# Two sets of split weights instead of three, and an expert unit held from the middle of the sections, in a one-layer mixer and mixture-of-experts kernel

## What is computed

```python
h  = RMSNorm(x) * (1 + scale_mix) + shift_mix          # scale, shift, gate from SiLU(c) @ w_ada
z  = h @ w_in              # [sc_x | sc_B | sc_C | u | v | gate_A | gate_B], 7 x 1024 columns
yA = sc_B * causal_dwconv3(sc_C * sc_x)
yB = GELU(u) * (tril(W_s) @_chunk LN(GELU(v)) + b_s)
x  = x + gate_mix * ((sigmoid(gate_A) * yA + sigmoid(gate_B) * yB) @ w_out)
h  = RMSNorm(x) * (1 + scale_ffn) + shift_ffn
x  = x + gate_ffn * MoE(h)         # top-4 of 32 experts, clamped SwiGLU, width 1024
```

## Time and profile before

| | before |
|---|---|
| median of 3 runs | 1135.45 us |
| the profiled execution's own time | 1135.09 us |
| its span, first to last instruction | 1133.3 us |
| granted TensorE clock, mean | 0.965 |
| PE busy / DVE busy / ACT busy | 960 / 369 / 230 us |
| moved by DMA, mean rate | 466.79 MB, 412 GB/s |

### The profile page before, as it was taken

The page is one execution under the profiler, slowest core; times in us unless marked ns, Lnnn a source line. Parts: engine busy times, 40 slices in busy tenths (PEclk is TensorE's granted clock), DMA queues, the critical chain, the costliest instruction groups (busy, mean ns, idle before and its releaser), DMA issues.

```text
span 1133.3 us, 24456 instructions
## 1 busy us (share of the span) xinstructions
PE 959.9 (85%) x10066; PEld 512.4 (45%) x10067; DVE 369.0 (33%) x844; ACT 230.4 (20%) x324; POOL 8.3 (1%) x30
## 2 busy tenths in 40 slices
PE   7999999998987897699798898988978688687665
PEld 5799999833332343243343333334333233233221
DVE  3688897642221221122221222212221121121112
ACT  3644534611110110011110111101110010010002
POOL 0010000000000000000000000000000000000000
PEclk9999999999999999999999999999999899899987
DMA  9999899999999999999999999999999999999996
GB/s 358 396 354 366 310 370 363 418 427 429 428 429 427 428 428 429 427 428 428 429 427 428 428 429 427 428 426 430 426 429 429 428 429 426 429 428 429 426 427 277
DMA packets 55854, 466.79 MB, mean 412 GB/s; under 512 B 4756, under 2 KB 5844, under 8 KB 27284
## 3 DMA queue, kind: packets, MB, share of 16 engines
q1 hardware_dynamic: 55568, 466.12, 99.1%
q10 hardware_dynamic: 260, 0.30, 0.1%
HBM read 465.35 MB, written 1.05 MB: 412 GB/s over the span
## 4 chain that ended last, share of the span: by engine, by line
PE 54%; DMA 37%; SPq 4%; issue 3%; DVE 1%; ACT 0%; DVEq 0%; another core or an unknown queue 0%; PEldq 0%; ACTq 0%
PE B L1530 26%; DMA trio<-in_w_down_dram 25%; PE B L1225 14%; DMA W<-in_w_down_dram 6%; DMA W<-in_w_gate_up_dram 4%; PE B L1554 3%; PE B L1479 2%; PE B L1543 2%; SPq L486 2%; SPq L490 1%; PE B L1304 1%; PE B L1485 1%; DMA raw<-in_w_ada_dram 1%; PE B L1255 1%; PE B L1313 1%
## 5 line engine op out<-in xcount | busy, mean ns | idle before, releaser
L1530 PE MATMUL B<-W,trio 128*32 128x512 f32 (+1 forms) x4768 | 470.8, 530 | 124.6 <-DMA W<-in_w_gate_up_dram 51.2
L1530 PEld LDWEIGHTS B<-W,trio 128*32 128x32 f32 x4768 | 155.6, 111 | 366.8 <-issue 222.4
L1155 DVE TENSOR_SCALAR EW<-B 128x256 f32<-128x256 f32 x46 | 19.5, 424 | 438.0 <-PE B L1530 438.0
L769 ACT ACTIVATE EW<-EW 128x256 f32<-128x256 f32 x46 | 19.2, 417 | 678.3 <-DVE EW L1155 678.3
L1225 PE MATMUL B<-hh,wh 128*128 128x256 f32 x384 | 109.1, 284 | 0.0
L1225 PE MATMUL B<-hl,wh 128*128 128x256 f32 x384 | 108.7, 283 | 0.0
L1225 PE MATMUL B<-hh,wl 128*128 128x256 f32 x384 | 108.6, 283 | 0.0
L1554 PE MATMUL B<-EW,trio 32*128 32x256 f32 x752 | 67.1, 426 | 8.7 <-PE B L1554 7.8
L1225 PEld LDWEIGHTS B<-hh,wh 128*128 128x128 f32 x384 | 73.7, 192 | 1.7 <-issue 0.8
L1172 DVE TENSOR_TENSOR EW<-B,trio 128x256 f32<-128x256 f32 x46 | 19.5, 424 | 166.6 <-PE B L1530 166.6
L1225 PEld LDWEIGHTS B<-hl,wh 128*128 128x128 f32 x384 | 73.7, 192 | 0.0
(11 more groups left out here) (257 smaller groups left out, 710.9 us busy)
## 6 DMA issues: line engine op xcount, KB each, us to landing
W<-in_w_gate_up_dram SPq DMA_DIRECT2D x112, 2048.0 KB, 34.2
W<-in_w_down_dram SPq DMA_DIRECT2D x48, 2048.0 KB, 37.3
spare<-in_w_gate_up_dram SPq DMA_DIRECT2D x16, 2048.0 KB, 37.1
trio<-in_w_down_dram SPq DMA_DIRECT2D x15, 2048.0 KB, 40.4
raw<-in_w_in_dram SPq DMA_DIRECT2D x10, 2048.0 KB, 13.8
raw<-in_w_ada_dram SPq DMA_DIRECT2D x4, 2048.0 KB, 18.3
raw<-in_w_ada_dram SPq DMA_DIRECT2D x6, 1024.0 KB, 12.1
raw<-in_w_in_dram SPq DMA_DIRECT2D x4, 1024.0 KB, 15.7
```

What stands on the lines that cost most here:

```text
L769: A(sg, gs, ACT.Sigmoid, scale=ALPHA).then_inc(sig_ready, 1)
L1155: V.tensor_scalar(halves(gs), paired(GU[:, 0:QC]), LIMIT, None, ALU.min).then_inc(gmin_ready, 1)
L1530: t = M(o, src[:, k % KQ, CAP * (k // KQ):CAP * (k // KQ) + CAP], w, start=(k == 0), stop=(k == KT - 1))
```

## The change

`SETS` becomes 2. The 16 KB a partition of the third set become a buffer `held`, which in the expert phase is slot 6 of `W`. The first expert unit u0 is loaded into it right after the unit `("in", SC_B, 1)` has been issued, with no wait of its own. All other early expert units move by one place in `PLACE`, each trigger now loads the unit with the next higher number into the same place as before, and the load that waited for `mix_done` 2 is gone (the third set's place is taken already). With two sets every split stands one iteration later against PE: iteration m splits piece m+2 instead of m+3; the piece that was split between the gelus and the squares of V is split in the loop; the split of section piece 1 waits for the whole V product; that of piece 26 waits for `mix_part` 1, that of piece 27 for `mix_done` 2.

```diff
-    SETS = 3
+    SETS = 2
+    HELD = 6
...
     def set_of(q):
-        return (q // 2) % SETS if q < V_ALL else (q - V_ALL + 1) % SETS
+        return (q // 2) % SETS if q < V_ALL else (q - V_ALL) % SETS
...
+            held = sb1("held", [P, UW])
...
-        SET_AT = [RING + set_of(len(piece_of) - 4 + i) for i in range(3)]
-        PLACE = (R2, R3, "spare", R1, R0, 8, 9, SET_AT[1], SET_AT[2], SET_AT[0], 7, "trio")
+        SET_AT = [RING + set_of(len(piece_of) - SETS + i) for i in range(SETS)]
+        PLACE = (HELD, R2, R3, "spare", R1, R0, 8, 9, SET_AT[0], SET_AT[1], 7, "trio")
...
         def set_free(eng, q):
...
-            elif t < 2:
-                eng.wait_ge(v_pair, t + 2)
-            elif t == 2:
+            elif t == 0:
+                eng.wait_ge(v_pair, 3)
+            elif t == 1:
                 eng.wait_ge(v_done, TA * NH)
             elif t < HALVES + SETS:
                 eng.wait_ge(sec_done, t - SETS + 1)
+            elif t == HALVES + SETS:
+                eng.wait_ge(mix_part, 1)
             else:
-                eng.wait_ge(mix_part, 1)
+                eng.wait_ge(mix_done, TA)
...
+                if n == unit_no[("in", SC_B, 1)]:
+                    load(0, 0)
...
             sp.wait_ge(ada_used, ada_units.index(unit_no[("half", 2, 5)]) + 1)
-            load(0, 0)
+            load(1, 0)
             sp.wait_ge(split_l, pieces_before[-4])
-            load(1, 0)
+            load(2, 0)
             sp.wait_ge(ada_used, len(ada_units))
             load_out_half()
             sp.wait_ge(ada_summed, NH)
-            load(2, 0)
+            load(3, 0)
             sp.wait_ge(split_l, pieces_before[-3])
-            load(3, 0)
+            load(4, 0)
             sp.wait_ge(split_l, pieces_before[-2])
-            load(4, 0)
+            load(5, 0)
             sp.wait_ge(sec_done, 2 * NS * NH)
-            load(5, 0)
+            load(6, 1)
             sp.wait_ge(m_ready, NH * 2)
-            load(6, 1)
-            sp.wait_ge(mix_done, TA)
             load(7, 1)
             sp.wait_ge(mix_part, 2)
             load(8, 1)
...
-            piece_high(V_ALL + 2)
             act.wait_ge(v_mu, 1)
...
-                        piece_high(V_ALL + m + 3)
+                        piece_high(V_ALL + m + SETS)
...
             m_high(1, 1)
+            piece_high(len(piece_of) - 2)
             piece_high(len(piece_of) - 1)
...
-            piece_low(V_ALL + 2)
             dve.wait_ge(v_sq, TA)
...
-                        piece_low(V_ALL + m + 3)
+                        piece_low(V_ALL + m + SETS)
...
             m_low(1, 1)
+            piece_low(len(piece_of) - 2)
             piece_low(len(piece_of) - 1)
```

More of the change, by code:

```diff
@@ L414, in _, with load @@
             sp.dma_start(x_sb[:, :, :], x_in[0].rearrange("(a p) n -> p a n", p=P)).then_inc(s_x, 16)
+            def load(u, e):
+                j = u % UNITS
+                if j < NQ:
+                    sp.dma_start(unit_pair(u).rearrange("p g n -> p (g n)"), gu_v[e, j]).then_inc(s_unit[u % SLOTS], 16)
+                elif PLACE[u % SLOTS] == "trio":
+                    sp.dma_start(unit_pair(u), dn_v[e, j - NQ]).then_inc(s_unit[u % SLOTS], 16)
+                else:
+                    sp.dma_start(unit_pair(u).rearrange("p g n -> p (g n)"),
+                                 dn_v[e, j - NQ].rearrange("p g n -> p (g n)")).then_inc(s_unit[u % SLOTS], 16)
             for n, (kind, s, h) in enumerate(units):
@@ L480, in load_out_half @@
                     sp.dma_start(to.rearrange("p (k n) -> p k n", n=HALF), out_v[:, 4 * c:4 * c + 4, HALF:2 * HALF]).then_inc(s_outw[c], 16)
[L482 to L493, removed]
+            assert [home(n) for n in (split_units[-4], split_units[-3], split_units[-2])] == [PLACE[i] for i in (2, 4, 5)]
             sp.wait_ge(ada_used, ada_units.index(unit_no[("half", 2, 5)]) + 1)
-            load(0, 0)
+            load(1, 0)
             sp.wait_ge(split_l, pieces_before[-4])
-            load(1, 0)
+            load(2, 0)
             sp.wait_ge(ada_used, len(ada_units))
```

## The result

The changed kernel took **1154.73 us** (median of 3 runs, 1154.29 to 1154.77) where the kernel before took 1135.45: a ratio of 1.0164 with an interval of 1.015 to 1.0178, or 19.3 us. The direction was forecast, the size was not: 1147.7 was forecast with a range up to 1151.5. The profiled execution took 1154.29 (span 1152.5).

The account below looks back on a forecast made before the run. DMA bytes were taken to set the pace from about 230 us, with PE's chain deciding when the stream starts. Terms (a) to (e), 2.5+0.6+3.7+4.0+1.5 = 12.3 us, on 1135.45 gave 1147.7, range 1142.5 to 1151.5.

Parts of the forecast that it names:

- (e): PE clock lowered after stalls: 1.5 us for work behind the tail's stall, bounds 0 and 1.6; nothing for the first stall.
- (a): Start of the sections: the splits of piece 2 stand behind gelus, squares and root, so PE stalls 2.5 us.
- Rival C: More stalls: first pieces and sections drop the clock too, late halves delay DVE; 4 us more, 1151.7; chance 0.12.
- (b): Before piece 12: DVE's gating and two weighings delay the low split; PE stalls 0.6 us, low 0.2, high 1.
- (c): Pieces 15 to 18: DVE's weighings and convolution work delay low splits; 3.7 us of stalls, between 2.8 and 4.2.
- (d): Tail: the split of piece 27 waits for `mix_done` 2, gates and residual pairs queue behind it; PE stalls 4.0 us.
- (f): The held unit's early 4.9 us of queue only moves the DMA hole: restart at 130.9 and not 125.07.
- (g): Load dropped at `mix_done` 2: queue runs dry near 231.5, PE chain sets the restart; first expert-released unit +12.3 us.
- B: The cover holds: PE never waits, DMA gains and losses net -1.0 to +0.7 us, 1135.4; chance 0.08.
- D: Stalls in the sections only: gates and DVE's tail work fit beside PE's product; 7 us, 1142.5; chance 0.10.

Follow-up runs that it names:

- run 3: Changed kernel with ACT's gate copies ahead of the splits of pieces 26 and 27, and DVE's low split of 27 behind its row work: 1152.56 us.
- run 2: Kernel before, three sets kept, but the first three pieces split under the changed kernel's conditions and order: 1140.52 us, ratio 1.0033.
- run 4: Changed kernel with 30 PE turns whose result nobody reads, ahead of the tail's wait for the residual pairs: 1150.53 us, ratio 1.0121.
- run 5: The changed kernel measured once more, with no edit: 1153.44 us, ratio 1.0164 against the kernel before.
- run 1: Kernel before, three sets kept, only the split of piece 27 waits for `mix_done` 2 and not `mix_part` 1: 1142.62 us, ratio 1.0057.
- run 8: Changed kernel with the held unit's load issued late, just ahead of the next unit's: 1153.11 us, ratio 1.0161.
- run 7: run 6 with high split 1 behind the gelus, high split 2 between squares and root, low ones alike: 1144.03 us, ratio 1.0076.
- run 9: run 7 with the last four half weighings one piece later on DVE: 1140.29 us, ratio 1.0038 against the kernel before.
- run 10: run 7 with DVE's weighings after the first cut to 16 or 64 columns, so it computes something else: 1136.64 us, ratio 1.0013.
- run 11: Kernel before, no held unit, with the load that followed `mix_done` 2 moved behind `mix_part` 2: 1139.05 us, ratio 1.0032.
- run 6: Changed kernel with the tail reordered: half the gate copies ahead of high split 26, half behind; DVE's tail work interleaved with its splits: 1147.38 us.

## Why the forecast had the direction and not the size

**The failed step is (e), the clock**, with the sentence "For the 2.5 us of (a) I take nothing; high end 1.5". The prediction took 1.5 us for a lower clock in all, with 3.0 to 3.1 as its own high end. The changed kernel loses 3.9 to it behind its stalls: 1.4 in the sections (155.31 us, against 153.87 in run 3 with the same stalls at full clock; run 2 has 1.7) and 2.4 after the tail's (17.3 us from the turns to the first expert, for 14.9; run 4 gets 2.3 back). Another 1.5 is lost at the start, which no edit explains, and 0.7 after the last landing.

The profiled execution is 19.2 over before's where 12.3 was forecast. The 6.9 between them are 2.4 of clock behind the stalls (3.9 less 1.5), 2.2 of longer stalls (13.0 by the starts of PE's matmuls, 8.6 and 4.35, for 10.8), 1.5 at the start, and 0.8 from the first expert's release to the end, 0.7 of it the clock in the last product of the kernel. With (e) right and nothing else changed the forecast would have been 1150.1, inside its range. The longer stalls carry that just past its end (1152.3), the start and the end of the kernel do the rest. The start's part is chance as far as the runs show; run 5, without it in its profiled execution, has 1153.44 and lies outside too.

For the tail the prediction took one early window that lost 1.55 us of its five. In run 1, with the same stall, that is the right size: 1.7. In the changed kernel the clock stayed down for longer, with 3.4 us lost over the window of 229 to 239 (0.66 of ten), 2.4 of it on work of PE; its second profiled execution and run 8 show the same (turns of 1.98 us in both). Why the same stall costs 1.7 in one kernel and 2.4 in the other stays open. For the first stall the prediction gave no reason to take nothing. Rival C ("the sections drop the clock too") had that mechanism, with 1151.7, and was given 0.12.

The other steps, one by one:

- (a) First pieces: 2.5 forecast, 2.74 by the row and 2.9 by the starts; run 2 has it alone, run 7 takes it away. Right in place and cause.
- (b) Piece 12: 0.6 forecast, 0.77 measured, within its bounds.
- (c) Pieces 15 to 18: 3.7 forecast as 0.6, 0.45, 0.6 and 2.1 to 2.4; measured 0.65, 0.71, 0.4 and 2.18, which is 3.9 by the brackets and 4.6 by the starts. The places are right; run 9 shows that the largest is the weighing at that place, run 10 that without DVE's bursts 0.3 is left of them. The one of 0.71 stands behind the half that landed late, as the prediction said it might.
- Sections in all: 6.8 forecast, 7.4 by the brackets and 8.6 by run 3, at full clock. Six times the 0.16 that a bracket leaves out is 1.0 of the difference. The product's start is 11.6 later: these 8.6, 1.4 of clock, and 1.5 from the start.
- (d) The tail: 4.0 forecast, 4.19 measured (4.35 by the starts), by the queue order that the prediction named. The rows of ACT and DVE in the changed kernel follow it: high 27, the gates behind it, and DVE between them.

```profile
220.30 1.92 ACT L649 ACTIVATE wh<-trio 128x2048 fp32r<-128x2048 f32 x1 [3.27 <-PE B L1229]
222.12 5.20 ACT L730 ACTIVATE tmp<-mod 32x512 f32<-32x512 f32 x8
...
222.25 2.29 DVE L851 TENSOR_TENSOR wl<-trio,wh 128x2048 fp32r<-128x2048 f32 x1 [2.89 <-ACT wh L649]
224.46 0.23 DVE L1018 COPY cols<-B 128x8 f32<-128x8 f32 x2
...
229.76 0.68 DVE L1046 TENSOR_TENSOR HV<-B,tmp 128x512 f32<-128x512 f32 x1
```

- (f) The hole moves and doesn't close: forecast restart 131, measured 134.56. The forecast moved it by one piece (5.8) and left out PE's own delay. That was 5.9 at the end of piece 11, and 3.7 of it came through. Run 8 can't tell the early load's worth from nothing, as forecast.
- (g) What the held unit saves is spent when the load of `mix_done` 2 is gone, and the chain sets the restart: the first load on the dry queue is issued at 238.9 and lands 8.9 later as forecast, and the stream is late by PE's lateness (+18.4 at both). Right; run 11 shows the price of a dry queue in a kernel with nothing else changed, 3.0 to 3.3, and run 10 that the two sides cancel when PE is nearly on time. The prediction's signs had the share of DMA low once more, near 232. It is low twice: 0.69 over 200 to 214, which isn't among them, and then from 234 on (0.13 over 234 to 240).

Of the rivals, B (the cover holds) is out by the seven stalls. Its account of the queue was good: run 10, in which the cover does hold, comes within 0.13% of before. The Trainium skill (Trainium Kernel Development and Optimization, Best Practices) says to double-buffer for performance. Here two buffers where three were cost 7.4 us of idle in the sections, by the waits: they were enough with DVE's bursts taken out (run 10, 0.3 us) and not with them. D (sections only) is out by the 4.19.

On the fixed cost of a transfer, the Trainium skill (DMA: Bandwidth & Descriptors, Anatomy of one DMA, SWDGE path) gives some 2.0 us over the bytes, for transfers that GpSimd issues. The prediction cites it without that condition, and the loads here are issued by SP. Measured, the one of 238.9 took 8.9 with 4.9 for its bytes, so 4.0 more; that of run 11, on a queue dry for 2 us, 7.84, so 2.9. Each had a second load issued 0.4 us behind it, so part of the surplus may be that load's share. For the landing the rows were the better guide.

What stays open: when a stall brings the clock down, and for how long. The first stall had the same 2.7 us in seven profiled executions (after, and runs 2, 3, 4, 5, 6 and 8); six show the lower clock behind it, that of run 3 doesn't, and that of run 4 shows twice the loss. The stall of 2.18 brought it down in run 4 alone.

## What to carry to other kernels

Before a buffer is taken away, add up the burst of each engine that fills it, not its average: the cover is the time between "may start" and "is wanted", and whatever stands in the same in-order queue counts against it. Price a stall of PE at its length and then at the half-speed work behind it (here 1.6 times the idle in both cases that were tried alone), and look at whether the stall can be filled or the queue reordered: the same new wait in the tail cost 6.5 us in one order of the queues, and another order gave 6.1 of them back. Filling a hole in the transfers early was worth nothing here, where the restart after the next hole hung on the compute chain.

## What the runs showed that was not expected

- The granted clock's loss after an idle PE is larger than the trace of before suggests: 1.4 to 1.7 us after 2.74 of idle (none in run 3, more in run 4), 1.7 (run 1) to 2.4 after 4.19. Thirty turns without use put into the second gave 2.3 back.
- It is not the same from run to run. Executions of the same kernel, or of two that are the same up to that point, differ by 1.5 us by 51 us on: 52.8 in two profiled executions, 50.8 to 51.4 in the others. In the windows it is seen as a granted clock of 0.83 from 20 to 30 us where the kernel before has this, with PE as busy and more matmuls recorded:

```profile
20.00:30.00 10.00, 9.07 (x47) 7.62 (x48) 8.59 (x14) 5.24 (x8) 0.00 (x0) 1.00 1.05 389
```

- Nor does the same stall always bring it down, or for as long. The stretch of 66 to 70 us, around the end of the first stall, in the changed kernel and then in run 3, which are alike up to there:

```profile
66.00:70.00 4.00, 2.78 (x13) 2.78 (x14) 3.89 (x3) 1.61 (x2) 0.00 (x0) 0.64 1.00 378
```

```profile
66.00:70.00 4.00, 4.00 (x36) 4.00 (x35) 3.86 (x3) 0.00 (x0) 0.00 (x0) 1.00 1.02 386
```

- The last product of the kernel (16 matmuls) takes 2.31 us in the changed kernel and 1.59 before; the whole time from the last landing to the end is 12.4 for 11.8. The windows from there to the end, of the changed kernel and then of before:

```profile
1140.00:1152.50 12.50, 3.24 (x32) 1.25 (x32) 3.74 (x9) 3.62 (x11) 0.00 (x0) 0.59 0.24 91
```

```profile
1121.50:1133.30 11.80, 2.50 (x32) 1.05 (x32) 3.74 (x9) 3.62 (x11) 0.00 (x0) 0.78 0.25 95
```

Nothing ties this to the change: the last product takes 1.59 us in runs 1, 3, 10 and 11 as well, and 2.25 to 2.63 in the other seven, run 2 with its three sets among them.

- A queue that is dry costs more than the time that it is dry before the issue: in run 11 that was 2 us, and 3.3 us were lost where the released unit lands.
